# Reordering a two-part weight projection: all slices with the high weights first, then all with the low ones

## The reference

```python
q, k, v, iq, ik, iw, za, u, zc, gt = in_project(h, w_in, ln_idx_g, ln_idx_b)
...
a_br = (attn * jax.nn.silu(za)) @ w_att_out
c_br = (jax.nn.silu(layer_norm(c, ln_conv_g, ln_conv_b)) * jax.nn.silu(zc)) @ w_conv_out
gate = jax.nn.sigmoid(gt.astype(jnp.float32)).astype(x.dtype)
mixed = gate[..., 0, :] * a_br + gate[..., 1, :] * c_br
return layer_norm(DEEPNORM_ALPHA * x + mixed @ w_o, ln_post_g, ln_post_b)
```

## Time and profile before

| | |
|---|---|
| median of three runs | 1671.73 us |
| the three runs | 1670.78, 1673.2, 1671.73 us |
| profiled execution: its own time | 1673.12 us |
| profiled execution: span, first to last instruction | 1671.3 us |
| mean granted TensorE clock | 0.993 of full |
| PE busy | 1632.1 us, 98% of the span |
| POOL, DVE, ACT busy | 609.5, 678.4 and 429.2 us |

### The profile page before, as it was taken

The page is one execution under the profiler, slowest core; times in us unless marked ns, Lnnn a source line. Parts: engine busy times, 40 slices in busy tenths (PEclk is TensorE's granted clock), DMA queues, the critical chain, the costliest instruction groups (busy, mean ns, idle before and its releaser), DMA issues.

```text
span 1671.3 us, 28144 instructions
## 1 busy us (share of the span) xinstructions
PE 1632.1 (98%) x10993; PEld 1518.4 (91%) x10993; DVE 678.4 (41%) x1624; ACT 429.2 (26%) x531; POOL 609.5 (36%) x182
## 2 busy tenths in 40 slices
PE   8999999999999999999999999999999999999995
PEld 6888489999999988899999999999999999988884
DVE  4022877432112101114888788706572222210018
ACT  4222622232332113221111221222361221231120
POOL 4244023432323232344544444555343333343330
PEclk9999899999999999999999999999999999999998
DMA  7333042233233443632223232233336444542213
GB/s 247 95 101 84 14 131 76 76 97 91 72 98 100 139 112 100 174 92 76 77 77 96 76 86 77 77 97 104 90 87 187 130 122 132 192 147 80 96 51 113
DMA packets 247373, 174.35 MB, mean 104 GB/s; under 512 B 17963, under 2 KB 224267, under 8 KB 246395
## 3 DMA queue, kind: packets, MB, share of 16 engines
q1 hardware_dynamic: 242635, 163.25, 34.3%
q10 hardware_dynamic: 4608, 9.44, 1.5%
HBM read 156.75 MB, written 16.63 MB: 104 GB/s over the span
## 4 chain that ended last, share of the span: by engine, by line
PE 94%; DVE 3%; issue 1%; ACT 1%; SPq 1%; POOL 0%; DMA 0%; DVEq 0%; POOLq 0%; ACTq 0%
PE ps L1531 72%; PE ps L1518 11%; PE ps L1574 2%; PE ps L1728 1%; PE ps L1737 1%; PE ps L1684 1%; PE ps L1515 1%; PE ps L1586 1%; PE ps L1514 1%; PE ps L1883 1%; DVE y L1478 1%; DVE y L1484 1%; PE ps L1702 1%; DVE bias L1185 1%; SPq L508 0%
## 5 line engine op out<-in xcount | busy, mean ns | idle before, releaser
L687 POOL TENSOR_TENSOR wlo<-raw,whi 128x2048 fp32r<-128x2048 f32 x115 | 531.2, 4619 | 901.7 <-ACT whi L778 901.7
L1531 PE MATMUL ps<-xhi,whi 128*128 128x288 f32 (+2 forms) x2912 | 648.5, 300 | 3.2 <-ACT tmp_tanh L984 2.2
L1531 PE MATMUL ps<-xlo,whi 128*128 128x288 f32 (+2 forms) x2912 | 646.4, 300 | 0.0
L1531 PE MATMUL ps<-xhi,wlo 128*128 128x288 f32 (+2 forms) x2912 | 642.4, 298 | 0.4 <-issue 0.4
L1531 PEld LDWEIGHTS ps<-xhi,whi 128*128 128x128 f32 x2912 | 470.9, 188 | 8.8 <-issue 2.5
L1531 PEld LDWEIGHTS ps<-xhi,wlo 128*128 128x128 f32 x2912 | 471.7, 188 | 3.0
L1531 PEld LDWEIGHTS ps<-xlo,whi 128*128 128x128 f32 x2912 | 471.4, 188 | 2.9
L778 ACT ACTIVATE whi<-raw 128x2048 fp32r<-128x2048 f32 x115 | 219.4, 1908 | 161.1 <-PE ps L1515 125.6
L1518 PE MATMUL ps<-whi,mixed 128*128 128x512 f32 x512 | 158.1, 390 | 0.5 <-POOL wlo L767 0.5
L1518 PEld LDWEIGHTS ps<-whi,mixed 128*128 128x128 f32 x512 | 95.8, 188 | 22.2 <-POOL wlo L767 1.8
L1369 DVE SCALAR_TENSOR_TENSOR ps<-U,dwT,ps 128x256 f32<-128x256 f32 x232 | 112.6, 485 | 0.0
(11 more groups left out here) (277 smaller groups left out, 1188.0 us busy)
## 6 DMA issues: line engine op xcount, KB each, us to landing
raw<-in_w_in_dram SPq DMA_DIRECT2D x83, 1024.0 KB, 5.7
raw<-in_w_o_dram SPq DMA_DIRECT2D x16, 1024.0 KB, 5.2
both_gates<-gates_dram SPq DMA_DIRECT2D x16, 576.0 KB, 6.7
raw<-in_w_att_out_dram SPq DMA_DIRECT2D x16, 512.0 KB, 4.2
raw<-in_w_conv_out_dram SPq DMA_DIRECT2D x16, 512.0 KB, 5.5
gates_dram<-tmp_gate ACTq DMA_DIRECT2D x24, 288.0 KB, 2.1
vpage<-in_cache_v_dram SPq DMA_DIRECT2D x32, 128.0 KB, 2.1
kpage<-in_cache_k_dram SPq DMA_DIRECT2D x32, 128.0 KB, 2.1
```

The costliest lines, as they stand in the source:

```text
L687: nc.gpsimd.tensor_tensor(wlo[:, buf, 0:width], raw[:, buf, 0:width], whi[:, buf, 0:width].bitcast(F32), ALU.subtract).then_inc(lo_ready, 1)
L1531: ins = mm(ps[:, bank + half, 0:width], w[b][:, k, :], x[:, k, t0 + half * width:t0 + (half + 1) * width], start=(k == k0 and m == 0), sto ...
```

## The change

`tile_block` ran, for each slice, the three products one behind the other. It now runs all slices with the high weights (`whi*xhi`, `whi*xlo`), and then all slices with the low weights (`wlo*xhi`). `one_tile` waits for the high half of the weights at the tile's start and, through the new argument `n`, for the low half between the two passes. The `each` signal stands in the second pass. The matmuls are the same in number and shape.

```diff
             def tile_block(buf, bank, k0=0, kn=KC, t0=META, width=OUTH, each=None, n=None):
 
                 w = [t[:, buf, :].rearrange("p (k c) -> p k c", k=KC) for t in (whi, wlo)]
+                parts = [(ps[:, bank + half, 0:width], slice(t0 + half * width, t0 + (half + 1) * width))
+                         for half in range((TOK - t0) // width)]
                 for k in range(k0, k0 + kn):
-                    for m, (b, x) in enumerate(((0, xhi), (0, xlo), (1, xhi))):
-                        for half in range((TOK - t0) // width):
-                            ins = mm(ps[:, bank + half, 0:width], w[b][:, k, :],
-                                     x[:, k, t0 + half * width:t0 + (half + 1) * width],
-                                     start=(k == k0 and m == 0), stop=(k == k0 + kn - 1 and m == 2))
+                    for m, x in enumerate((xhi, xlo)):
+                        for out, cols in parts:
+                            mm(out, w[0][:, k, :], x[:, k, cols], start=(k == k0 and m == 0), stop=False)
+                if n is not None:
+                    block_ready(n)
+                for k in range(k0, k0 + kn):
+                    for out, cols in parts:
+                        ins = mm(out, w[1][:, k, :], xhi[:, k, cols], start=False, stop=(k == k0 + kn - 1))
                     if each is not None and k < k0 + kn - 1:
                         ins.then_inc(each, 1)
                 return ins
 
             def one_tile(n0, b, i=0, **cols):
...
-                block_ready(n + i * 2)
-
+                pe.wait_ge(hi_ready, n + 1 + i * 2)
                 pe.wait_ge(tile_taken, n - C_OF + 1 + i * 2)
...
-                tile_block(n % 2, 2 * b, **cols).then_inc(block_used, 1)
+                tile_block(n % 2, 2 * b, n=n + i * 2, **cols).then_inc(block_used, 1)
```

More of the change, by code:

```diff
@@ L1523, in rows_block, with tile_block @@
                         ins.then_inc(out_sem, 1)
-            def tile_block(buf, bank, k0=0, kn=KC, t0=META, width=OUTH, each=None):
+            def tile_block(buf, bank, k0=0, kn=KC, t0=META, width=OUTH, each=None, n=None):
                 w = [t[:, buf, :].rearrange("p (k c) -> p k c", k=KC) for t in (whi, wlo)]
+                parts = [(ps[:, bank + half, 0:width], slice(t0 + half * width, t0 + (half + 1) * width))
+                         for half in range((TOK - t0) // width)]
                 for k in range(k0, k0 + kn):
-                    for m, (b, x) in enumerate(((0, xhi), (0, xlo), (1, xhi))):
-                        for half in range((TOK - t0) // width):
-                            ins = mm(ps[:, bank + half, 0:width], w[b][:, k, :],
-                                     x[:, k, t0 + half * width:t0 + (half + 1) * width],
-                                     start=(k == k0 and m == 0), stop=(k == k0 + kn - 1 and m == 2))
+                    for m, x in enumerate((xhi, xlo)):
[6 more added lines that the diff above has]
+                        ins = mm(out, w[1][:, k, :], xhi[:, k, cols], start=False, stop=(k == k0 + kn - 1))
                     if each is not None and k < k0 + kn - 1:
```

## The result

The changed kernel takes 1678.8 us (median of 6 runs, 1677.99 to 1680.89), the kernel before 1672.47 us (6 runs, 1670.78 to 1673.45) on the same chip. The ratio is 1.0041, with an interval of [1.0028, 1.0054]: slower by 0.41%, 6.3 us between the medians. The forecast was 1676.0, 4.3 us more than before, in a range up to 1678.3; the measured time lies 0.5 us above the range. The profiled execution took 1678.74 us, 5.62 more than that of before (1673.12), and its span is 5.6 longer.

A forecast was written before the change was run, and what follows sets the result against it. The prediction took PE, busy 98% of the span, as the bound. Three terms of 0 plus 1.2 us at block 85 and 3.1 at block 87 made 4.3 us over the 1671.73 median: 1676.0 us, range 1671.8 to 1678.3.

The forecast's parts named there:

- The low wait in the middle, and one more wait: Projection tiles: moving the low-weight wait to mid-tile gains 0, and one more wait in each of 80 tiles costs 0.
- the rival in which the waits cost after all: 80 tiles: a mid-tile wait uncovers one weight load, 189 ns each, 15 us, 1687 us (1691 with the hand-over); chance 0.06.
- The order of the matmuls: All tiles and branch blocks: running the passes in the new order costs 0, pairs still following each other at 0.26 us.
- Steps 1 and 2: Block 84 frees its first slice at 1240.73; ACT then splits block 86 at 1250.4 and starts the 16th slice at 1252.2.
- Step 3: POOL's split of block 86 starts at 1252.4 and shuts DVE out; the 16th xlo is written at 1257.65.
- the rival in which the hand-over stays nearly hidden: 16th xlo: DVE gets in before POOL or runs beside it, or POOL starts behind DVE; 0.3 to 0.9 us lost; chance 0.16.
- Step 4: Block 85: PE reaches slice 15 at 1256.43 and waits until 1257.65, 1.2 us.
- Step 5: Gates issued 7.2 us later, block 87's split ends at 1274.2 and not by 1269.9: total 4.3 us, 3.1 at block 87.
- the last sentence of step 5: Behind block 87: block 88 is ready about 1281 and due at 1286.9, so nothing more is lost and nothing given back.

The follow-up runs named there:

- experiment 1: Two kernels: the changed kernel with block 84 alone in the old order, 1672.93 us; the kernel before with only block 84 in two passes, 1678.07 us.
- experiment 2: The changed kernel, but ACT writes the 16th slice of xhi before the late gate and the split of block 86: 1673.89 us, ratio 1.0015.
- experiment 3: Changed kernel, block 84 in old order, low weights awaited at each tile's start: 1673.65 us. Where the 16th slice is named, experiment 2 is the run that fits.
- experiment 7: Changed kernel, block 87's weights loaded ahead of the gates and split ahead of mhi(0), with 8.4 us of ACT copies before that split: 1678.94 us.
- experiment 6: The kernel before with added ACT copies making one gap ahead of block 87: gap 1.0 us, 1673.85 us; 2.1 us, 1675.39 us; 3.3 us, 1677.97 us.
- experiment 8: The kernel of experiment 2 with 4.3 us of ACT copies ahead of block 87's split: 1677.56 us, ratio 1.004.
- experiment 4: The changed kernel, but SP issues the weights of block 87 ahead of the gates: 1676.55 us, ratio 1.0028.
- experiment 10: The kernel of experiment 3, but in the high pass the xlo products run one slice behind the xhi ones: 1674.02 us, ratio 1.0009.

## Why the prediction was wrong

**The direction and where the waits come from** were right: experiments 1 and 2 put the loss into block 84's hand-over, and experiment 3 into the 16th slice.

**The low wait in the middle, and one more wait: 0.** Right: 1.0009 and 1.0011 with the wait in the middle and at the start. With it falls the rival in which the waits cost after all, at the price of a weight load in each of 80 tiles.

**The order of the matmuls: 0.** Wrong by a little, and the row under it was too narrow. The order costs nothing in the early tiles: between ACT's takings of eight results (237.53 to 326.75 us before, 235.61 to 324.88 after) a tile takes 12.75 us in both. But in blocks 77 to 84 and in the branches the old order runs at 12.69 us and the new one at 12.75, about 1 us in all (23 tiles). I had read the pairs at 0.26 us, which can't tell 132.2 from 132.8 ns a matmul. Why the old order is faster there and not in the early tiles stays open.

**Steps 1 and 2** gave the first slice at 1240.73, the split of block 86 at 1250.4 and the 16th slice at 1252.2. Measured: 1240.42, 1250.14, 1251.96. Block 84 started 0.31 us earlier than in the profile before (1231.53, not 1231.84); with that taken off, steps 1 to 3 are met within 0.1 us.

**Step 3** gave POOL's start at 1252.4 and the 16th `xlo` at 1257.65. Measured, in order of time:

```profile
1252.13 4.60 POOL L687 TENSOR_TENSOR wlo<-raw,whi 128x2048 fp32r<-128x2048 f32 x1 [12.80 <-ACT whi L778]
1252.66 4.69 DVE L1424 TENSOR_TENSOR xlo<-zc,xhi 128x576 fp32r<-128x576 f32 x1 [1.40 <-ACT xhi L1078]
1257.41 0.52 PE L1888 MATMUL ps<-xhi,whi 128*128 128x288 f32 x2 [1.22 <-DVE xlo L1424]
```

DVE ends at 1257.35, 0.62 us behind POOL, as before. The rival in which the hand-over stays nearly hidden falls with this: POOL wins, by 0.53 us.

**Step 4**, 1.2 us in block 85: right, 1.22.

**Step 5**, 3.1 us ahead of block 87: too much by 1.1. The gates were issued at 1257.45, which is my 1257.75 less the 0.3 us of the earlier start. But the second load of block 87, issued at 1258.88, landed after 7.66 us where I had taken 8.4, the longest of the earlier trace rows, so ACT's split began 0.7 us sooner than by my steps. And PE came to block 87 some 0.4 us later than I had it, in part because blocks 84 and 86 took 12.75 us.

**The step that failed is the last sentence of step 5**, that with no gap in the chain "nothing more is lost", and the sum with it: I costed the gaps by their own length. A gap can cost more than it lasts. Behind the second one the granted clock is at the lower level, and the first matmuls of block 87 pay 1.8 us: 6.03 us for 32 of them, not 4.25. All four profiles with a gap of 2.0 to 2.4 us ahead of block 87 and one of 1.2 us in block 85 have it: two of the changed kernel and one each of experiments 1 (second kernel) and 7. None of the six with a gap of 2.1 to 3.3 us ahead of block 87 and none of 1.2 before it (experiments 6 and 8) has it, nor that with gaps of 1.2 and 1.5 (experiment 4). Yet that it takes two gaps is not shown, and as a rule it is wrong: behind the lone gap at 904 us the clock falls in six of 19 profiles. What decides whether a given gap brings the clock down stays open; its length and a gap ahead of it do not settle it.

**Luck.** 4.3 with the 1.8 on top would be 6.1, close to the measured 6.3. But that is two errors against each other: step 5 had the gap 1.1 us too long, and the order of the passes, put at 0, costs about 1.

The sum corrected: 1.2 + 2.0 + 1.8 for the hand-over, and about 1 for the order of the passes; 6.0 against 6.3 of the medians and 5.6 of the profiles.

## What to carry to other kernels

Where a loop is reordered inside a tile, look for signals that hang on its middle: nearly all of this loss came from the one tile of 80 whose slices are released to another engine, and only because an instruction that had come before a POOL instruction now came behind it. Count a gap on PE by its length and by the clock behind it, and take more than one profile before you say that a gap leaves the clock alone. And in a two-part product keep one moving operand for a whole pass: three passes instead of alternation gave 0.34% here, more than both new waits together.

## What the runs showed of the hardware

- **The clock behind a gap.** PE at the lower clock for some 3.4 us behind a gap of 2.0 to 2.4 us: in all four profiles where it stands ahead of block 87, some 14 us behind one of 1.2, and in six of 19 where it stands alone at 904 us; full clock behind it in the other 13, and in the profiles behind single gaps of 2.1, 2.3 and 3.3 us ahead of block 87. The Trainium skill, in "TensorE: Matmul & The Clock Gate", section "🔬 Part 1: The HAM clock gate (the "warmup" mystery)", has it that an idle TensorE falls back to half its clock. The rows agree in kind, with 0.57 granted, and show that the length of a gap alone doesn't decide.
- **Changing the moving operand.** 131.7 ns a matmul with one operand through the pass (8.43 us for 64), 133.3 with `xhi` and `xlo` in turn (8.53), whether a weight block is used four times in a row (experiment 3) or twice (experiment 10).
- **A wait that is met** between two matmuls has no cost that shows: with 80 of them at the tiles' starts or in their middles the ratios are 1.0011 and 1.0009, and the tiles take 12.75 us in both.
- **DVE and POOL.** DVE's two-operand instruction of 0.75 us takes 4.69 when POOL starts 0.53 us ahead of it. Four such instructions take 2.76 us together where they end before POOL starts (experiment 2).
